# Gates of the first block's merges: sigmoid table on the scalar engine in place of exp, plus one and reciprocal

## What is computed

```python
xn = rmsnorm(h, norm_g[l])
(a_q, ..., g_a, g_b, g_c) = split_cols(xn @ w_in[l])
y_a = hgrn2_mixer(...)
y_b = mlstm_mixer(...)
y_c = rwkv7_mixer(...)
merged = (jax.nn.sigmoid(g_a) * (y_a @ w_br[l, 0])
          + jax.nn.sigmoid(g_b) * (y_b @ w_br[l, 1])
          + jax.nn.sigmoid(g_c) * (y_c @ w_br[l, 2]))
h = h + merged @ w_out[l]
```

## Time and profile before

| what | value |
|---|---|
| median of 3 runs | 3409.15 us (3408.1 to 3411.21) |
| the profiled execution's own time | 3415.68 us |
| its span, first to last instruction | 3413.9 us |
| mean granted PE clock | 0.994 of full speed |
| PE / PEld busy | 3379.4 / 2949.7 us |
| DVE busy | 1577.5 us |
| ACT busy | 639.8 us |
| POOL busy | 45.0 us |
| gate read-outs, L495 | 48, 383 ns each, from 259.0 to 1409.1 us of the span |

### The profile page before, as it was taken

The page is one execution under the profiler, slowest core; times in us unless marked ns, Lnnn a source line. Parts: engine busy times, 40 slices in busy tenths (PEclk is TensorE's granted clock), DMA queues, the critical chain, the costliest instruction groups (busy, mean ns, idle before and its releaser), DMA issues.

```text
span 3413.9 us, 53363 instructions
## 1 busy us (share of the span) xinstructions
PE 3379.4 (99%) x22582; PEld 2949.7 (86%) x22582; DVE 1577.5 (46%) x2834; ACT 639.8 (19%) x1632; POOL 45.0 (1%) x83
## 2 busy tenths in 40 slices
PE   9999999999999999999999999999999999999999
PEld 7888888888888898888899997877779999988787
DVE  2426631324556471522455756524344566563343
ACT  1012200011011000111111216412131112352211
POOL 1000000000000000000000000000000000000000
PEclk9999999999999999999999999999999999999999
DMA  7443244433444302553444444333444544533432
GB/s 233 136 152 114 100 148 147 149 124 112 154 128 144 99 4 70 203 170 104 141 156 149 157 149 139 87 124 118 142 128 148 166 148 157 173 124 87 145 127 74
DMA packets 436422, 454.89 MB, mean 133 GB/s; under 512 B 25307, under 2 KB 412832, under 8 KB 435904
## 3 DMA queue, kind: packets, MB, share of 16 engines
q1 hardware_dynamic: 433600, 444.48, 41.1%
q0 software_dynamic: 2128, 5.19, 0.5%
q10 hardware_dynamic: 464, 1.90, 0.1%
HBM read 449.46 MB, written 2.10 MB: 132 GB/s over the span
## 4 chain that ended last, share of the span: by engine, by line
PE 98%; DVE 1%; ACT 0%; DVEq 0%; issue 0%; POOL 0%; ACTq 0%; POOLq 0%
PE bank L367 21%; PE bank L289 19%; PE bank L2063 10%; PE bank L481 10%; PE bank L1952 9%; PE bank L307 5%; PE bank L515 5%; PE bank L2127 3%; PE bank L1602 3%; PE bank L1162 3%; PE bank L2036 1%; PE bank L2114 1%; PE bank L2086 1%; PE bank L544 0%; PE bank L1989 0%; PE bank L687 0%
## 5 line engine op out<-in xcount | busy, mean ns | idle before, releaser
L289 PE MATMUL bank<-xnT,ring 128*128 128x272 f32 (+1 forms) x2816 | 633.2, 388 | 1.6 <-ACT wk L912 1.0
L289 PEld LDWEIGHTS bank<-xnT,ring 128*128 128x128 f32 x2816 | 535.2, 190 | 99.2 <-issue 3.3
L481 PE MATMUL bank<-xnT,ring 128*128 128x256 f32 x1536 | 343.7, 383 | 0.7 <-ACT wk L1336 0.7
L367 PE MATMUL bank<-xnT,ring 128*128 128x128 f32 (+1 forms) x2688 | 332.4, 281 | 0.0
L481 PEld LDWEIGHTS bank<-xnT,ring 128*128 128x128 f32 x1536 | 290.7, 191 | 40.9 <-ACT wk L1336 1.1
L1952 PE MATMUL bank<-xnT,ring 128*128 128x272 f32 (+2 forms) x1408 | 325.7, 390 | 0.0
L367 PEld LDWEIGHTS bank<-xnT,ring 128*128 128x128 f32 x2688 | 323.1, 191 | 1.0 <-issue 0.9
L1952 PEld LDWEIGHTS bank<-xnT,ring 128*128 128x128 f32 (+1 forms) x1408 | 260.5, 187 | 51.4 <-issue 0.7
L2063 PE MATMUL bank<-G,ring 128*128 128x272 f32 (+1 forms) x1024 | 239.4, 388 | 0.0
L367 PE MATMUL bank<-G,ring 128*128 128x128 f32 (+1 forms) x1792 | 225.3, 279 | 0.0
L2063 PEld LDWEIGHTS bank<-G,ring 128*128 128x128 f32 x1024 | 191.7, 190 | 35.7 <-issue 3.6
(11 more groups left out here) (563 smaller groups left out, 3791.0 us busy)
## 6 DMA issues: line engine op xcount, KB each, us to landing
ring<-in_w_in SPq DMA_DIRECT2D x155, 2048.0 KB, 8.3
ring<-in_w_out SPq DMA_DIRECT2D x32, 2048.0 KB, 8.3
ring<-in_w_br SPq DMA_DIRECT2D x12, 2048.0 KB, 8.9
ring<-in_w_out SPq DMA_DIRECT2D x16, 1024.0 KB, 10.7
ring<-in_w_in SPq DMA_DIRECT2D x8, 512.0 KB, 6.9
G<-in_x POOLq DMA_DIRECT2D x2, 1024.0 KB, 8.6
wk<-in_pool_w POOLq DMA_DIRECT2D x2, 1024.0 KB, 9.1
out<-G SPq DMA_DIRECT2D x8, 256.0 KB, 2.6
```

Of the source, the lines that this page charges most:

```text
L289: mm = pe.matmul(bank[j][:, first:T], ring[:, s, k, j * P:(j + 1) * P], rhs[:, k, first:T], start=(k == 0), stop=(k == KT - 1))
L367: mm = pe.matmul(out_, weights[:, k, :], x(k), start=(start and k == 0), stop=(k == HALF - 1), skip_group_check=True)
L481: mm = pe.matmul(bank[j][:, META:T], ring[:, s, k, j * P:(j + 1) * P], xnT[:, k, META:T], start=(k == 0), stop=(k == KT - 1))
```

## The change

In the first block, the read-out of a gate tile computes Sigmoid(g) instead of exp(-g), and the merges drop the plus one and the reciprocal, with the drain after each. The order of all other instructions, the transfers, the semaphores and the products are as they were.

```diff
@@ gates_act @@
                 act.wait_ge(proj_full, tiles["act"].go())
-                act.activation(hT[:, t % KT, META:T], bank[t % 2][:, META:T], ACT.Exp, scale=-1.0).then_inc(proj_free, 1)
+                act.activation(hT[:, t % KT, META:T], bank[t % 2][:, META:T], ACT.Sigmoid).then_inc(proj_free, 1)
@@ merge_dve @@
                     gate, dst = hT[:, bass.ds(i * 4 + j, 1), META:T], merged[:, bass.ds(i * 4 + j, 1), META:T]
-                    v.tensor_scalar(gate, gate, 1.0, None, ALU.add)
-                    v.drain()
-                    v.reciprocal(gate, gate)
-                    v.drain()
                     v.wait_ge(br_full, i * 4 + (KT * b + j + 1))
```

## The result

The changed kernel takes 3421.53 us (median of 7 runs, 3416.62 to 3423.98), the kernel before 3408.1 us beside it (3404.43 to 3411.21). The ratio is 1.0037, with a 95% interval of 1.0027 to 1.0047: slower by 0.27 to 0.47%, which is about 9 to 16 us. The forecast of no change was wrong, and 3421.5 lies outside its range.

The account below looks back on a forecast made before the run. PE was taken to bound the kernel, so other engines' work counts only through PE's waits. Removed work 0 plus added loads 0 left 3409.2 us against the median (profiled 3415.68), range 3406 to 3414.5.

Parts of the forecast that it names:

- What bounds the kernel: Whole kernel: PE, busy 3379.4 of 3413.9 us; DVE or ACT work counts only by what PE waits for it.
- What is removed is worth nothing: Merges: 97.9 us of DVE's plus one and reciprocal are hidden behind PE's products; value 0.
- 34 loads of 1.28 us, ACT near 683 us, DVE near 1480: First block's three mixers: switches between Sigmoid and Exp add 43.6 us of ACT; removed merge work lowers DVE from 1577.5.
- A load is thus done in ACT's idle time ahead of the wait: Table loads at levels, heads and gates: each runs before its instruction's wait, as at the third mixer's Ln; cost 0.
- the sum of 0: Whole change: 0 for the removed DVE work plus 0 for the added table loads, so the time stays.
- Rival A: Levels: a switch holds ACT about twice the load, exps late by 0 to 1.11 us; 4 us, 3413; chance 0.07.
- Rival B: Nine levels: loads lie behind the waits, PE waits longer for DVE; 8.8 us, 3418, bound 11.5 us; chance 0.07.
- A delay of any size: Rival B's deciding point: an exp delayed by any amount at the levels where PE waits now.
- Rival C: Removed DVE work was on the path somewhere: faster, 3404.6 us at best, still under 0.2%; chance 0.03.
- rival D: Program gets fewer loads, from a table with both functions: same 3409.2 us, only ACT's busy time tells; chance 0.03.

Follow-up runs that it names:

- e4: Kernel before without plus one and reciprocal in the merges, gates left as exp(-g), so only its time is of use: 3408.4 us, ratio 0.9999.
- e3: Changed kernel with the two waits of each level swapped, PE's scores named first and DVE's sums last: 3407.8 us, ratio 0.9999 to the kernel before.
- e2: Changed kernel with the exp table asked for ahead of the two waits of each level: 3409.1 us, ratio 1.0000 to the kernel before.
- e1: The changed kernel run again with no edit: 3417.9 us, ratio 1.0031 to the kernel before.
- e6: Kernel before with two table loads (sigmoid, then exp) behind the two waits of each level: 3427.4 us, ratio 1.0055.
- e5: Kernel before, gates still exp, with the sigmoid table asked for ahead of each level's waits, so exp's is reloaded: 3418.7 us, ratio 1.0029.
- e7: Kernel before with six one-column copies on ACT behind the two waits of each level, no table load: 3410.0 us, ratio 1.0003.

## Why the prediction was wrong, point by point

- **What bounds the kernel: right.** PE's waits were the view to go by, and the cost appeared there.
- **What is removed is worth nothing: right.** e4 measured it by itself at 0.9999, and the end of the third merge has about the same idle PE. DVE's waits for the merges' products (L515) grew from 24.1 to 139.3 us, by 115 us where nearly 97.9 was expected: the freed time went there (the rest is probably the 13.5 us that L524 had waited for gates).
- **34 loads of 1.28 us, ACT near 683 us, DVE near 1480: right.** They were 34, 684.4 and 1482.4 us. One of the 34 lies on L339 and not on L907 as forecast; no wait of PE grew there. Gates with two waits of their own (the first of the second and third branch) were read out 1.3 us late, and no one waited.
- **"A load is thus done in ACT's idle time ahead of the wait": this is the step that failed.** The price of the loads at the levels was put at 0, and they cost 10.2 us. The step was taken from the earlier trace rows, one load whose function has one wait, and carried over to the levels, whose exp has two. It held at the heads (L921: 0.1 us of idle time before four loads), not at the levels (29.6 us before nine). For the levels the prediction did consider that the load might stand behind one of the waits, but took it to be the first, DVE's sums. It was the other, PE's scores. e3 shows that with DVE's sums there the sum of 0 would have been right.
- **Rival A, a dearer switch: fell.** e2 has every switch and no cost. By the Trainium skill (ScalarE: Activation LUTs, "What ACT_TABLE_LOAD costs") the drain would have added about 1.38 us a switch. In after, a head's exp waits 0.29 us for DVE behind a load that began 0.02 us behind the gate: gate's end to exp is 1.60 us, too short for 2.66.
- **Rival B, loads behind the waits: this is what happened,** at a chance of 0.07, which was too little for the doubt that the prediction itself named. Its place was right: PE's wait for the banks that DVE takes out behind its second sum. Its price of 8.8 us was near. At levels with no slow tile ahead of them the stalls grew by 1.16 to 1.32 us at six levels (two of these read from e1) and by 0.86 and 0.89 us at two, 9.3 us together; this sum is an estimate from the two traces. In after only 6.4 us of it shows, because two slow tiles gave DVE time and took the stalls of the second and fifth level away. The slower clock was missing from the price altogether, and so were 0.5 us among the scores. But the clock adds little: a slow tile costs 1.6 to 1.7 us and takes away the next stall, wholly (after) or in part (e6). The levels are 9.8 us longer with one slow tile (e1), 10.2 with two (after) and 10.8 with three (e5). "A delay of any size" held in the trace of e7, where 0.57 us of delay became 0.6 us more stall.
- **Rival C fell** (e4), and of **rival D** there is no sign.

## What to carry to other kernels

Where a change of function brings table loads, count them, but cost them by where they land: in idle time a load of 1.28 us is free, nine of them inside a chain of dependent steps cost 10 us here. With two waits in front of the function, look in the built program for the one that stands in front of the load; name the wait that ends first last, or ask for the table by hand ahead of both. And a row that shows how the build places something is evidence for instructions of that form, with that number of waits, and for no others.

## What the runs showed of the hardware that was not expected

**Behind a stall of PE the next products can run at half the clock.** Stalls of 1.01 and 1.06 us (e7) and of 0.3 to 0.5 us (before) left the gate tile at 7.17 us. In after, behind a stall of 1.73 and one of 1.57 us, tiles took 8.77 and 8.86 us, the first with a granted clock of 0.50 for some 3 us. It doesn't happen every time. In the same execution another stall of 1.57 us left its tile at 7.17 us. In e1 the tile behind the first stall of 1.73 us took 7.17 us and the one behind the second 8.86 us:

```profile
306.11 0.33 PE L683 MATMUL bank<-G 128*32 128x32 f32 x16 [1.73 <-DVE merged L765]
...
307.64 7.17 PE L481 MATMUL bank<-xnT,ring 128*128 128x256 f32 x32
...
318.91 8.86 PE L481 MATMUL bank<-xnT,ring 128*128 128x256 f32 x32
```

Neither the length of the stall nor the weight transfers decide between the two. In e5 a tile of 8.73 us came behind a stall of 1.33 us, and in e6 one of 7.17 us behind a stall of 2.48 us. And the second slow tile of after ran at a granted clock of 0.50 with no transfer at all, while the first tile of e1 had the full clock under heavy transfers (stretches as above; first line after, second e1):

```profile
342.00:343.00 1.00, 1.00 (x4) 0.50 0.00 0
```

```profile
308.00:309.00 1.00, 1.00 (x6) 1.00 1.09 364
```

What does decide wasn't settled.

**The rest of the span varies by 12 us** over the ten profiled executions (3312.7 to 3324.5 us), though little that PE waits for changed there. Some of it is the same fall of the clock at other places: from 1186 to 1300 us the kernel before had a granted clock of 0.94, and after had 0.98 in about the same stretch; between the fourth and the fifth gate of the third mixer it took 5.4 us less (106.3 against 111.7):

```profile
1186.00:1300.00 114.00, 112.75 (x3035) 0.94 0.07 22
```

```profile
1197.00:1304.00 107.00, 105.99 (x2992) 0.98 0.08 23
```

The first line is of the kernel before, the second of after. This spread is as large as the effect, which is why two profiled executions of equal length hid a change of 0.3%, and only the time between two marks around the levels showed it.
